# Hybrid decoder step on one core: POOL computes the S5 output matrices as soon as the powers are there, beside the input kernel on DVE

## What is computed

```python
def s5_mixer(u, a_re, a_im, log_dt, b_re, b_im, c_re, c_im, d_skip, ...):
    dt = jnp.exp(log_dt)
    mag = jnp.exp(a_re * dt)
    lr, li = mag * jnp.cos(a_im * dt), mag * jnp.sin(a_im * dt)   # lambda, one complex number per state
    ...                                                           # cr, ci: the input scale
    bbr = cr[..., None] * br - ci[..., None] * bi                 # complex input matrix
    bbi = cr[..., None] * bi + ci[..., None] * br
    xr = jnp.einsum('blgh,gph->blgp', uf, bbr)
    xi = jnp.einsum('blgh,gph->blgp', uf, bbi)
    _, _, sr, si = lax.associative_scan(combine, (lr, li, xr, xi), axis=1)
    y = einsum(sr, c_re) - einsum(si, c_im) + d_skip * uf
```

## Time and profile before

| | |
|---|---|
| median of 3 runs | 1498.5 us (1498.1 to 1499.82) |
| the profiled execution: time | 1499.42 us |
| the profiled execution: span, first to last instruction | 1497.6 us |
| granted TensorE clock, mean over the span | 0.943 of full |
| PE busy | 1424.6 us (95%) |
| DVE busy | 664.5 us (44%) |
| ACT busy | 432.4 us (29%) |
| POOL busy | 146.7 us (10%) |

### The profile page before, as it was taken

How to read it: one execution, slowest core, us unless ns; L and a number is a source line. 1 busy time by engine, 2 the same in 40 slices (tenths; PEclk the granted TensorE clock), 3 DMA queues, 4 the chain that set the end, 5 groups by cost and what they waited for, 6 DMA issues and landing times. The chain is left out here.

```text
span 1497.6 us, 25204 instructions
## 1 busy us (share of the span) xinstructions
PE 1424.6 (95%) x10400; PEld 1331.4 (89%) x10400; DVE 664.5 (44%) x910; ACT 432.4 (29%) x667; POOL 146.7 (10%) x140
## 2 busy tenths in 40 slices
PE   6677999789999999999999999999999999999998
PEld 5676676459999999999998888889999999999998
DVE  3935432436544422444555344337754442344432
ACT  6121212333422211222224244445232221122211
POOL 2590000004200000000230000000500000000000
PEclk9789556989999999999999999999999999999999
DMA  5272100312433331333322121212333233222332
GB/s 151 65 85 51 70 1 8 81 50 81 136 91 91 100 97 57 93 88 89 97 68 72 44 59 46 58 45 71 100 105 92 84 105 91 70 85 84 95 97 80
DMA packets 242168, 117.30 MB, mean 78 GB/s; under 512 B 45060, under 2 KB 237528, under 8 KB 242088
## 3 DMA queue, kind: packets, MB, share of 16 engines
q1 hardware_dynamic: 237576, 116.15, 28.1%
q10 hardware_dynamic: 4528, 0.24, 0.2%
HBM read 108.03 MB, written 8.16 MB: 78 GB/s over the span
## 5 line engine op out<-in xcount | busy, mean ns | idle before, releaser
L315 PE MATMUL ps<-xh,whi 128*128 128x272 f32 x1408 | 291.7, 288 | 2.0 <-DVE wlo L274 2.0
L315 PE MATMUL ps<-xh,wlo 128*128 128x272 f32 x1408 | 291.4, 288 | 0.0
L315 PE MATMUL ps<-xl,whi 128*128 128x272 f32 x1408 | 290.3, 288 | 0.0
L315 PEld LDWEIGHTS ps<-xh,whi 128*128 128x128 f32 x1408 | 221.5, 188 | 2.6 <-issue 2.5
L315 PEld LDWEIGHTS ps<-xl,whi 128*128 128x128 f32 x1408 | 221.2, 188 | 0.0
L315 PEld LDWEIGHTS ps<-xh,wlo 128*128 128x128 f32 x1408 | 219.8, 189 | 0.0
L274 DVE TENSOR_TENSOR wlo<-wraw,whi 128x1024 fp32r<-128x1024 f32 (+1 forms) x118 | 165.1, 1399 | 98.3 <-ACT whi L269 93.9
L269 ACT CAST whi<-wraw 128x1024 fp32r<-128x1024 f32 (+1 forms) x118 | 133.1, 1128 | 139.5 <-PE ps L315 139.5
L315 PE MATMUL ps<-hh,whi 128*128 128x272 f32 x704 | 145.7, 288 | 0.0
L315 PE MATMUL ps<-hl,whi 128*128 128x272 f32 x704 | 145.5, 288 | 0.0
L315 PE MATMUL ps<-hh,wlo 128*128 128x272 f32 x704 | 145.4, 288 | 0.0
(11 more groups left out here) (507 smaller groups left out, 2087.6 us busy)
## 6 DMA issues: line engine op xcount, KB each, us to landing
wraw<-in_w_gate SPq DMA_DIRECT2D x88, 256.0 KB, 3.0
wraw<-in_w_up SPq DMA_DIRECT2D x88, 256.0 KB, 3.0
wraw<-in_w_down SPq DMA_DIRECT2D x32, 384.0 KB, 3.7
wraw<-in_w_in_odd SPq DMA_DIRECT2D x48, 256.0 KB, 3.1
wraw<-in_w_down SPq DMA_DIRECT2D x32, 320.0 KB, 3.1
wraw<-in_w_in_even SPq DMA_DIRECT2D x20, 256.0 KB, 4.2
wraw<-in_w_out_odd SPq DMA_DIRECT2D x16, 256.0 KB, 3.1
ev_xs<-in_x_prompt SPq DMA_DIRECT2D x2, 1024.0 KB, 6.6
```

The costliest lines, as they stand in the source:

```text
L315: ins = pe.matmul(K.ps[:, 2 * s + h, 0:HT], w[s][:, k, :], a[:, k, h * HT:(h + 1) * HT], start=start, stop=stop)
```

## The change

DVE no longer waits for `npw`, but signals a new semaphore `powers` with it. POOL starts `F` on that semaphore, where it waited for the sixth operation of `eb`. Nothing else is changed: the operations, their operands and their order on each engine stay.

```diff
-        "sinv", "diag", "bc", "rms", "c_t", "ct", "bb", "pw", "eb", ...
+        "sinv", "diag", "bc", "rms", "c_t", "ct", "bb", "pw", "powers", "eb", ...
@@ DVE
-        st(dve.tensor_scalar(npw[:], pw[1][:], -1.0, None, ALU.mult), sw)
-        st.sync()
+        dve.tensor_scalar(npw[:], pw[1][:], -1.0, None, ALU.mult).then_inc(S["powers"], 1)
         panel_end(1)
@@ POOL
-        pool.wait_ge(S["eb"], 6)
+        pool.wait_ge(S["powers"], 1)
         pool.wait_ge(S["ct"], 4)
```

More of the change, by code:

```diff
@@ L583, in phase_even @@
         "const", "par_in", "gn_in", "x_in", "x_in2", "s5_in", "tab", "par_t", "gn_t", "gains", "small", "act", "x_t", "stat", "sln",
-        "sinv", "diag", "bc", "rms", "c_t", "ct", "bb", "pw", "eb", "uz", "et", "e", "u_out", "u_in", "xpe", "xsb", "rot", "f", "ktp",
+        "sinv", "diag", "bc", "rms", "c_t", "ct", "bb", "pw", "powers", "eb", "uz", "et", "e", "u_out", "u_in", "xpe", "xsb", "rot", "f", "ktp",
         "ktc", "ktd", "zero", "g_in", "h_in", "h_t", "h0", "hz", "r", "scan", "h", "dec", "fin", "fin_t", "fin_sb", "hx", "ype", "ysb", "yd",
```

## The result

The changed kernel takes 1513.78 us (median of 4 runs, 1513.54 to 1514.18) against 1498.85 (1498.1 to 1499.82): a ratio of 1.01, 95% interval 1.0082 to 1.0117, so slower by 14.9 us. The profiled execution of it has a span of 1511.7 us against 1497.6, 14.1 more.

The account below looks back on a forecast made before the run. DVE's work ahead of L1469, the end of eb at 77.47, was taken to set the pace. Turns of 15.2 less 0.1 behind gave 15.1 on the profiled 1499.4, so 1514.5, or 1513.6 against the median; range 1504 to 1518.

Parts of the forecast that it names:

- strict turns: DVE and POOL alternate on the SBUF port up to L1469: 15.2 us there, median 1513.6; likeliest case, chance 0.61.
- 1: DVE's removed wait for `npw`, after L1451: cost next to nothing, taken as 0.
- step 2: Start of F on POOL: about 59.75 instead of 77.56, one dispatch after L1451 ends at 59.67.
- 3: DVE from panel 1's evacuation to L1469: eight exclusive operations wait for POOL, 15.2 us; L1469 ends near 92.7.
- 4: Path behind L1469: panel 5's L615 nets -0.1, SP's transfers move by 15.1, ACT's by 15.2.
- the clock rival: PE's clock stays at 1.2 GHz through the second transposes: up to 7.5 us more, 1521.1; chance 0.10.
- 5: What F gives back: it ends near 103, but nobody waits for it before U lands: 0.
- the list of signs: Expected in the changed profile, including PE's wait before the first transposes grown to 10 us and more.
- DVE keeps the port over consecutive operations: Rival up to L1469: POOL gets in only in DVE's gaps, sum 6.7 us, 1505.2; chance 0.17.
- POOL yields: Rival up to L1469: DVE wins every contest, only 1.2 us lost, 1499.1 to 1499.7; chance 0.08.
- the transfers swallow 7.1 us: Rival at U's landing: the transfers' own rate sets it, so 8.1 us remain of 15.2, 1506.6; chance 0.04.

Follow-up runs that it names:

- the run with DVE late: Kernel before, with four 128x2304 memsets on DVE ahead of L1469 and POOL idle beside them: 1509.38 us, ratio 1.0065.
- the run with `F` still later: Kernel before, but F starts only behind the low part of panel 5 (80.20 instead of 77.56): 1499.62 us, ratio 0.999.
- the run with the memsets: Changed kernel, but from `powers` POOL only does fourteen 128x1152 memsets, and F is computed after eb: 1499.03 us, ratio 0.9998.
- the run with two doublings later: Kernel before, with the last two doublings of POOL's rotation factors (twelve operations) put behind eb, ahead of F: 1495.71 us, ratio 0.9977.

## Why the prediction was right

The median was forecast at 1513.6 and is 1513.8, and the likeliest case, strict turns, is the one that happened. The steps, in its numbering:

1. The removed wait was taken as 0. It is 0.12 us: the evacuation now begins 0.08 before L1451 ends, where it began 0.04 after.
2. POOL was to start at 59.75, 0.08 after L1451, and starts 0.09 after, at 60.59, released by `npw`. L1451 itself came 0.83 us later than in the other execution. That is no effect of the change: the operations ahead of it are the same, and the lateness is there long before. PE's batch of four transposes (L764) at 21.00 takes 1.05 us, where the same batch at 20.50 takes 0.60 in the kernel before, and by 40.23 DVE is 1.0 behind (39.22 before); 0.2 of it comes back where the powers meet POOL's rotation work. In the other runs with the same order up to there L1451 ends between 59.59 and 61.57, and in the latest of them, the run with DVE late, two such batches are long. Why a batch is long in one execution and not in another is not shown: the granted clock reads 1.00 there in all three.
3. The eight turns, forecast and measured as growth over the undisturbed 1.21 or 2.29: L615 1.2 and 1.22; L1460 2.0 and 1.94; L1461 2.0 and 1.95; L1463 2.5 and 2.31; L615 1.0 and 1.00; L1466 2.5 and 2.44; L1467 2.0 and 1.94; L1469 2.0 and 1.82. Together 15.2 and 14.6. Both kinds of POOL operation were priced a little high. The first 1.2 is right by two errors that cancel: with L615 ending 1.08 after POOL's operation, as the rows had it, the forecast's own times give 1.1, but the evacuation ended 0.1 sooner behind L1451 than it assumed.
4. The path behind was to pass on 15.1. The L615 of panel 5 takes 1.57 instead of the 1.80 of before (1.7 was argued). `eb` moved by 15.3 (0.8 from step 2, 14.5 from 1 and 3), `U` by 14.9, the first kernel row by 14.1. The last 0.7 come from PE's clock: after the wait for `U` the granted clock is low for less time, so that panel 6 gets its short matmuls (0.41 for two) again from 118.72, 3.4 us after the wait's end, where it was 5.1 before. Ahead of that the clock did the opposite, and a small part of the clock rival came true: the first transposes take 3.68 instead of 3.17 and the short matmuls are back 5.6 us after that wait's end instead of 4.2, so the second batch (1.91 as before) starts 10.3 us after the first instead of 9.4, and ACT's transfers go out 16.2 later, not 15.2. That cost nothing at `U`, which moved by 14.9, SP's transfers by 15.1. The length of the wait alone doesn't explain it: behind waits of 3.5 us the first batch takes 2.46 in the run with `F` still later, 3.17 before, and 3.67 in the run with the memsets.
5. `F` ends at 103.38 (forecast near 103) and brings nothing; the run with `F` still later confirms that its start doesn't matter.

So the closeness of the total is in part luck: 0.6 too much for the turns and 1.1 too much behind them are partly set off by the 0.8 of the start, which has nothing to do with the change. The profiled executions differ by 0.8 less than the medians do (14.1 and 14.9), and the median of before is now 1498.85 where the forecast counted from 1498.5. The mechanism, eight strict turns on a path almost without slack, is what the timeline shows. One thing was forecast wrong in the list of signs: PE's wait ahead of the first transposes grew to 7.62, not to over 10. The other part, 8.15, stands ahead of panel 4, whose low part was late too, and which then ran at a low granted clock.

The rivals: that DVE keeps the port over consecutive operations happened in none of the turns. The behaviour of the earlier trace rows exists, but here DVE had always just waited itself when its next operation came; that this is what decides was argued from the rows and not tried. That POOL yields is refuted by the timeline. That the transfers swallow 7.1 us is refuted by it and by the run with DVE late; they swallow 0.4 and 1.6. What was argued of the port from a handful of rows is now shown from both sides: memsets on POOL free, copies on POOL not, a PSUM operand on DVE free.

## What to carry to other kernels

Work put on POOL beside DVE was free here where POOL didn't read SBUF, or where DVE's two-operand operation took one operand from PSUM. Otherwise each DVE operation on the path was charged about the length of one POOL operation, so look for what DVE has on the path in that stretch, and for slack of the moved work's reader, before moving it. Where it must overlap, cut POOL's operations short (half the length, less than half the loss here) or put one operand of DVE's in PSUM.

Don't read this as "one SBUF operand on DVE is safe". A copy from SBUF to SBUF has one and waits in the kernel before:

```profile
48.85 0.68 DVE L1444 COPY s_pw_r<-s_small 128x16 f32<-128x16 f32 x1
```

```profile
47.85 1.63 POOL L405 TENSOR_TENSOR s_rot_r<-s_rot_r,ssum 128x256 f32<-128x256 f32 x1
```

The copy ends at 49.53, POOL's operation at 49.48. In the run with two doublings later, with POOL idle, the same copy takes 0.16.

And read the same rule backwards on the kernel as it stands: POOL work that nobody waits for, running beside DVE work that somebody does, can be put off, which was worth 5 us here.

## What the runs showed of the hardware that was not expected

When PE's clock comes back can differ between executions by more than many edits are worth, in a stage far behind the change. The profiled execution of the run with `F` still later took 1507.89 us, though its median is 1499.62. Its first kernel row is at 122.91 and POOL's last attention copy at 199.48, where the kernel before has 123.05 and 199.94; then its first square of the residual comes at 355.01 against 345.66. Busy time by stage, that run first, then the kernel before; the columns are the stage, the busy time (and instructions) of PE, PEld, DVE, ACT and POOL, the granted clock as a share of full, DMA share and GB/s:

```profile
200.00:250.00 50.00, 50.00 (x154) 36.23 (x155) 13.43 (x34) 11.19 (x43) 0.26 (x1) 0.50 0.00 0
250.00:300.00 50.00, 42.69 (x148) 26.28 (x148) 17.14 (x35) 12.61 (x46) 0.00 (x0) 0.73 0.27 66
```

```profile
200.00:250.00 50.00, 50.00 (x155) 36.30 (x155) 13.44 (x34) 11.17 (x43) 0.72 (x2) 0.50 0.00 0
250.00:300.00 50.00, 41.08 (x175) 24.54 (x173) 20.16 (x44) 18.94 (x56) 0.00 (x0) 0.91 0.27 66
```

Both run at 1.2 GHz from 200 to 250 us with PE busy all the time, and have the same work to do. The kernel before gets 2.4 GHz back near 252 us, the other only after 266 (0.73 against 0.91 over the 50 us from 250), and it is 9.4 us behind at the first square. The profiled execution with two doublings put off shows the same: it is 8.3 us ahead of the kernel before at the first kernel row, but stays at 0.50 until 260 us, and its time is 8.5 us above the fastest of its own kernel. That could hide the 1.8 us that it gained at `U`, but no trace of a faster execution of that kernel is there to show it. What decides when the clock comes back was not tried.
